# Two transformer blocks on one core: the second block's q, k, conv and gate panels as seven block products ahead of the attention, the conv projection as the attention's filler

## The reference, cut to what matters

```python
h = modulate(rms_norm_2(x, g_pre_mix[l]), sh1, sc1)
proj = h @ w_in[l]                                   # 1024 x 5120
bg, cg, u, q, k, v, ga, gb = jnp.split(proj, split_pts, axis=-1)   # 512 x6, 1024 x2
y_conv = short_conv_branch(bg, cg, u, conv_w[l]) @ w_proj_conv[l]  # bg * conv3(cg * u)
o = stick_breaking_attention(q, k, v)                # 8 heads of 64
y_attn = o @ w_proj_attn[l]
merged = jax.nn.sigmoid(ga) * y_conv + jax.nn.sigmoid(gb) * y_attn
mix_out = merged @ w_out[l]
```

## Time and profile before

| | |
|---|---|
| Median of 3 runs | 2811.23 us |
| Profiled run, and its span | 2811.8 us, 2810.0 us |
| PE busy | 96% of the span, 15746 matmuls |
| DVE, ACT, POOL busy | 62%, 41%, 19% |
| Entry of the second block | 1381.7 to 1471.2 us |
| Attention with filler | 1471.2 to 1879.8 us |
| Gates and projections | 1879.8 to 2059.4 us |

### The profile page before, as it was taken

How to read it: one execution, slowest core, us unless ns; L and a number is a source line. 1 busy time by engine, 2 the same in 40 slices (tenths; PEclk the granted TensorE clock), 3 DMA queues, 4 the chain that set the end, 5 groups by cost and what they waited for, 6 DMA issues and landing times.

```text
span 2810.0 us, 39071 instructions
## 1 busy us (share of the span) xinstructions
PE 2688.0 (96%) x15746; PEld 2169.7 (77%) x15746; DVE 1731.8 (62%) x1998; ACT 1139.4 (41%) x2138; POOL 541.7 (19%) x434
## 2 busy tenths in 40 slices
...
GB/s 134 59 31 18 7 4 24 3 25 178 93 202 188 210 170 193 111 87 99 148 55 46 38 46 31 66 80 51 75 198 102 111 100 120 120 150 120 120 105 120
DMA packets 222604, 269.50 MB, mean 96 GB/s; under 512 B 16455, under 2 KB 158046, under 8 KB 222430
## 3 DMA queue, kind: packets, MB, share of 16 engines
...
...
## 4 chain that ended last, share of the span: by engine, by line
PE 80%; DVE 10%; POOL 3%; ACT 2%; issue 2%; DMA 2%; SPq 0%; ACTq 0%; DVEq 0%; POOLq 0%
PE ps L1647 7%; PE ps L1648 7%; PE ps L1649 7%; PE ps L1702 5%; PE ps L1704 5%; PE ps L1703 5%; PE ps L1761 4%; PE ps L1217 3%; PE ps L1219 3%; PE ps L1218 3%; PE ps L1763 3%; PE ps L1762 3%; PE ps L1438 3%; PE ps L1344 2%; PE ps L1236 1%
## 5 line engine op out<-in xcount | busy, mean ns | idle before, releaser
L1702 PE MATMUL ps<-down_t_hi,down_s_hi 128*128 128x512 f32 x896 | 349.5, 390 | 4.4 <-DVE acc L3205 2.2
L1704 PE MATMUL ps<-down_t_hi,down_s_lo 128*128 128x512 f32 x896 | 348.7, 389 | 0.0
L1703 PE MATMUL ps<-down_t_lo,down_s_hi 128*128 128x512 f32 x896 | 348.6, 389 | 0.0
L1043 POOL TENSOR_SCALAR mean_sq<-ssq 128x1 f32<-128x1 f32 x64 | 37.1, 580 | 1294.7 <-ACT squares_junk_ffn L1921 1242.2
L428 POOL TENSOR_TENSOR slab_lo<-raw,slab_hi 128x1024 fp32r<-128x1024 f32 (+2 forms) x108 | 256.1, 2371 | 9.0
L2385 ACT CAST down_s_hi<-down_a 128x2048 fp32r<-128x2048 f32 x56 | 107.2, 1915 | 370.4 <-PE ps L1704 328.1
L425 POOL TENSOR_SCALAR slab_hi<-raw 128x1024 fp32r<-128x1024 f32 (+2 forms) x108 | 114.6, 1061 | 624.0 <-issue 479.6
L1647 PE MATMUL ps<-act_hi,up_hi 128*128 128x512 f32 (+1 forms) x544 | 205.7, 378 | 6.1 <-issue 2.8
L1648 PE MATMUL ps<-act_lo,up_hi 128*128 128x512 f32 (+1 forms) x544 | 204.9, 377 | 0.0
L1649 PE MATMUL ps<-act_hi,up_lo 128*128 128x512 f32 (+1 forms) x544 | 204.8, 376 | 0.0
L1702 PEld LDWEIGHTS ps<-down_t_hi,down_s_hi 128*128 128x128 f32 x896 | 168.2, 188 | 42.6 <-issue 8.0
...
## 6 DMA issues: line engine op xcount, KB each, us to landing
down_a<-hid_spill SPq DMA_DIRECT2D x32, 1024.0 KB, 7.3
hid_spill<-up_hid ACTq DMA_DIRECT2D x30, 1024.0 KB, 6.4
raw<-in_w_in SPq DMA_DIRECT2D x56, 512.0 KB, 3.8
w_ada<-in_w_ada SPq DMA_DIRECT2D x48, 512.0 KB, 3.9
raw<-in_w_out SPq DMA_DIRECT2D x32, 512.0 KB, 3.8
up_raw<-in_w_up SPq DMA_DIRECT2D x16, 1024.0 KB, 5.4
down_b<-in_w_down SPq DMA_DIRECT2D x16, 1024.0 KB, 6.9
up_raw<-in_w_mlp_in SPq DMA_DIRECT2D x16, 1024.0 KB, 5.4
```

What stands on the lines that cost most here:

```text
L1702: pe.matmul(out, ops["s_hi"][:, k, cols], ops["t_hi"][:, k, :], start=first, stop=False, skip_group_check=True)
L1703: pe.matmul(out, ops["s_hi"][:, k, cols], ops["t_lo"][:, k, :], start=False, stop=False, skip_group_check=True)
L1704: mm = pe.matmul(out, ops["s_lo"][:, k, cols], ops["t_hi"][:, k, :], start=False, stop=last, skip_group_check=True)
```

## The change

The q, k, conv and both gate projections (36 panels, before spread over three stages) become 18 steps of two panels, `IN_COLUMNS`. Each step is seven products of four units (`in_product`), all of them ahead of the attention and behind v. ACT and DVE prepare the weight combinations (`in_high`, `in_low`, `in_add`), six products ahead (`IN_AHEAD`), instead of POOL. Within a step the order is 5, 6, 2, 7 (`UP_FIRST`), with product 1 two places earlier and products 4 and 3 behind the next step's first. The results go to DRAM (`in_d`, `v_d`) and come back for the attention and the merge. The convolution's taps run on DVE inside steps 6 and 7 and steps 9 and 10. The attention's filler is now the conv projection alone (`fill_unit`, 64 units, one for each step from step 10 on); turns alternate between two PSUM banks. After the attention only the attention projection is left.

The diff, cut to PE's, SP's and POOL's parts (`base` columns, orders, loads, products, filler):

```diff
+IN_FIRST = (1, 2, 6, 5, 7)
+IN_COLUMNS = [base + 2 * P * n for base in (IN2_Q, IN2_K) for n in range(2)]
+IN_COLUMNS += [base + 2 * P * n for n in range(2) for base in (CONV2, 2 * CONV2, 0)]
+IN_COLUMNS += [base + 2 * P * n for base in (IN2_GA, IN2_GB) for n in range(4)]
+IN_STEPS = len(IN_COLUMNS)
+IN_CONV, IN_GATES = 4, 10
+IN_KEPT = [u for u in range(IN_STEPS) if not IN_CONV <= u < IN_GATES]
...
+def in_order():
+
+    order = [(0, p) for p in IN_FIRST]
+    for u in range(1, IN_STEPS):
+        order += [(u, 1), (u - 1, 4), (u - 1, 3)] + [(u, p) for p in UP_FIRST[1:]]
+    return order + [(IN_STEPS - 1, 4), (IN_STEPS - 1, 3)]
+
+
+IN_ORDER = in_order()
+IN_TOTAL = len(IN_ORDER)
...
+IN_AHEAD = 6
...
+FILL_FIRST = 10
+FILL_UNITS = KD * 2 * CONV2_PANELS
+FILL_IN_STEPS = FILL_UNITS - 2 * CONV2_PANELS
+
+
+def fill_first_unit(step):
+
+    return min(max(step - FILL_FIRST, 0), FILL_IN_STEPS)
...
-        R5 = Ring(sem, MID_FIRST + len(MID_PANELS), raws[:3], slab_hi[:3], slab_lo[:3], R3)
-        R9 = Ring(sem, 3 * KD, raws[:2], slab_hi[:2], slab_lo[:2], R5)
+        R5 = Ring(sem, 4, raws[:3], slab_hi, slab_lo, R3)
+        R9 = Ring(sem, 2 * KD, raw_half, half_hi, half_lo, R5)
...
+            def in_load(u):
+
+                sp.dma_start(up_raw[u % 2][:], w_in2[:, :, IN_COLUMNS[u]:IN_COLUMNS[u] + 2 * P]).then_inc(sem(f"in_raw{u % 2}"), 16)
...
+            def qkv_loads(i, done):
+
+                for to, src in ((q2[i], in_d[i]), (k2[i], in_d[SB_PAIRS + i])):
+                    sp.dma_start(to[:], src).then_inc(sem(done), 16)
+                sp.dma_start(v2[i][:], v_d[:, :, i * P:(i + 1) * P].rearrange("t p (h e) -> p t h e", e=SB_DIM)).then_inc(sem(done), 16)
...
+            sp.wait_ge(R5.split_done, R5.SLOTS + R5.base + R5.total)
+            in_load(0)
+            sp.wait_ge(sem("v_stored"), FROM["v_stored"] + 32)
+            in_load(1)
+            for u in range(2, IN_STEPS):
+                sp.wait_ge(sem("in_lo"), FROM["in_lo"] + IN_AT[u - 2, 4] + 1)
+                in_load(u)
+            sp.wait_ge(sem("y_stored"), FROM["y_stored"] + 32)
+            for u in (0, 1, 2, 3):
+                in_stored(sp, u)
+            sp.wait_ge(sem("in_lo"), FROM["in_lo"] + IN_AT[IN_STEPS - 2, 4] + 1)
+            qkv_loads(0, "qk_first")
+            for p in range(2):
+                R9.load(sp, 0, p, narrow_view, w_pc[:, :, p * P:(p + 1) * P])
+            sp.wait_ge(sem("in_prod"), FROM["in_prod"] + IN_TOTAL)
             sp.dma_start(y_in[:], y_d.rearrange("c p n -> p c n")).then_inc(sem("y_in"), 16)
...
+            for u in range(IN_GATES, IN_STEPS):
+                in_stored(sp, u)
...
+            for p in range(2):
+                conv_gate_load(p)
+            for i in range(1, SB_PAIRS):
+                qkv_loads(i, "qk_in")
...
+            R5.split(pool, 0, 1, 3)
+            for u in IN_KEPT[-2:]:
+                in_stored(pool, u)
...
+            t_turn("n3", 0, range(KD))
...
+            def v2_part(h, j):
+
+                R5.ready(pe, 0, j)
+                if j == 0 and h == 0:
+                    pe.wait_ge(sem("down_taken"), FROM["down_taken"] + 2 * DOWN_TOTAL)
+                pe.wait_ge(sem("turn_split"), TURNS["n3"] + h * KD + 2 * j + 2)
+                for t in range(4):
...
+            for j in range(3):
+                v2_part(0, j)
+            pe.wait_ge(sem("turn_read"), TURNS["n3"] + KD)
+            t_turn("n3", 1, range(4))
+            v2_part(0, 3)
+            t_turn("n3", 1, range(4, KD))
+            for j in range(4):
+                v2_part(1, j)
...
+            def in_product(n):
+
+                u, p = IN_ORDER[n]
+                slot, b = n % UP_SLOTS, in_bank(u, p)
+                pe.wait_ge(sem("in_lo"), FROM["in_lo"] + n + 1)
+                if u == 0:
+                    if p in (4, 5, 6, 7):
+                        pe.wait_ge(sem("it_lo"), FROM["it_lo"] + IN_T_AT[1, p])
+                    if p in (1, 2, 5):
+                        pe.wait_ge(sem("v2_done"), {1: 5, 2: 6, 5: 7}[p])
...
+                elif p in (6, 7, 4):
+                    pe.wait_ge(sem("in_copied"), FROM["in_copied"] + IN_COPY_AT[u, {6: 1, 7: 6, 4: 7}[p]])
...
+                for k in range(4):
+                    hi, lo = (t_moving(p, w, k) for w in range(2))
+                    pe.matmul(out, up_hi[slot][:, k, :], hi, start=(p in (1, 2, 5) and k == 0), stop=False, skip_group_check=True)
+                    pe.matmul(out, up_hi[slot][:, k, :], lo, start=False, stop=False, skip_group_check=True)
+                    mm = pe.matmul(out, up_lo[slot][:, k, :], hi, start=False, stop=(k == 3), skip_group_check=True)
+                mm.then_inc(sem("in_prod"), 1)
+
+            for n in range(IN_TOTAL):
+                in_product(n)
+
+            def fill_unit(m):
+
+                n, k = divmod(m, CONV2_PANELS)
+                p, h = divmod(n, 2)
+                if m == 0:
+                    pe.wait_ge(sem("c2_split"), CONV2_PANELS)
+                if k == 0 and h == 0:
+                    R9.ready(pe, 0, p)
+                if k == 0 and n:
+                    fill_done(pe, n - 1)
...
+                pe.matmul(ps[:, 5, :], half_hi[p % 2][:, w], y_hi[:, k, cols], start=(k == 0), stop=False)
+                pe.matmul(ps[:, 5, :], half_hi[p % 2][:, w], y_lo[:, k, cols], start=False, stop=False)
+                mm = pe.matmul(ps[:, 5, :], half_lo[p % 2][:, w], y_hi[:, k, cols], start=False, stop=(k == CONV2_PANELS - 1))
...
+                if step >= SB_LAG_TURN:
+                    sb_turn(*divmod(step - SB_LAG_TURN, SB_ITEMS))
...
-                mid_units(unit, end)
+                for m in range(fill_first_unit(step), fill_first_unit(step + 1)):
+                    fill_unit(m)
...
+            for m in range(FILL_IN_STEPS, FILL_IN_STEPS + 2):
+                fill_unit(m)
+            sb_outputs(SB_PAIRS - 1, NT - 1)
+            for m in range(FILL_IN_STEPS + 2, FILL_UNITS):
+                fill_unit(m)
```

and ACT's, DVE's parts:

```diff
+            def in_high(n):
+
+                u, p = IN_ORDER[n]
+                in_slot_free(act, n)
+                if p in (1, 2, 4):
+                    in_loaded(act, u)
+                else:
+                    act.wait_ge(sem("in_sum"), FROM["in_sum"] + IN_SUM_AT[u, p])
+                act.copy(up_hi[n % UP_SLOTS][:], in_source(u, p)).then_inc(sem("in_hi"), 1)
...
+            def v2_take(h):
+
+                for t in range(4 * h, 4 * h + 4):
+                    if t < NT - 1:
+                        act.wait_ge(sem("v2_prod"), t + 1)
+                    else:
+                        R5.panel_done(act, 0, 3)
+                    act.copy(v2_out[h][:, t % 4, :], ps[:, t % 4 if h else 4 + t, :]).then_inc(sem("v2_done"), 1)
+                act.wait_ge(sem("v2_done"), 4 * h + 4)
+                act.dma_start(v_d[4 * h:4 * h + 4].rearrange("t p n -> p t n"), v2_out[h][:]).then_inc(sem("v_stored"), 16)
...
+            v2_take(0)
+            for p in (7, 6, 4):
+                it_hi(1, p)
+            for n in range(4):
+                in_high(n)
+            act.preload_act_table_set("sigmoid_and_others")
+            v2_take(1)
+            for h in range(2):
+                it_hi(h, 5)
+            for n in range(4, IN_AHEAD):
+                in_high(n)
+
...
+            def in_store(u):
+
+                act.wait_ge(sem("in_copied"), FROM["in_copied"] + IN_COPY_AT[u, 4])
+                act.wait_ge(sem("in_out"), FROM["in_out"] + max(IN_OUT_AT[u, p] for p in (2, 5, 3)))
+                if u >= IN_GATES:
+                    act.activation(hid_cols(u, 1, 1), hid_cols(u, 1, 1), ACT.Sigmoid)
+                    act.activation(up_hid[u % 2][:, 0, :], up_hid[u % 2][:, 0, :], ACT.Sigmoid).then_inc(sem("in_gated"), 1)
+                    act.wait_ge(sem("in_gated"), FROM["in_gated"] + u - IN_GATES + 1)
+                act.dma_start(in_d[2 * u:2 * u + 2].rearrange("j p c -> p j c"), up_hid[u % 2][:]).then_inc(sem(f"in_stored{u % 2}"), 16)
...
+            for n, (u, p) in enumerate(IN_ORDER):
+                if p in (1, 6, 7, 4):
+                    in_copy(u, p)
+                if p == 6 and u - 1 in IN_KEPT:
+                    in_store(u - 1)
+                for g in range(2):
+                    if (u, p) == (IN_CONV + 3 * g + 4, 1):
+                        conv_store(g)
+                if n + IN_AHEAD < IN_TOTAL:
+                    in_high(n + IN_AHEAD)
...
+            for u in IN_KEPT[-2:]:
+                in_stored(act, u)
+            for step in range(SB_STEPS + SB_LAG_TURN):
                 sb_step(step)
...
+            for n, (u, p) in enumerate(IN_ORDER):
+                if n and IN_ORDER[n - 1][1] in OUT_AFTER:
+                    in_output(IN_ORDER[n - 1][0], OUT_AFTER[IN_ORDER[n - 1][1]])
+                for x in in_sums(n + IN_AHEAD + 1):
+                    in_add(*x)
+                if n + IN_AHEAD - 1 < IN_TOTAL:
+                    in_low(n + IN_AHEAD - 1)
+                conv_part(u, p)
```

(3 more changed lines are left out.)

654 lines of the change are left out of this document (330 added, 324 removed).

## The result

The changed kernel takes 2821.5 us (median of 7 runs, 2817.98 to 2825.58), the kernel before 2810.86 us in the same comparison. The ratio is 1.0036, with a 95% interval of 1.0026 to 1.0047: slower by 0.36%, 10.6 us. The forecast was 2820.0 us.

What follows compares the result with a forecast made beforehand. PE was taken to bound the kernel, busy 96% of the span. Terms -49.0 + 1.7 + 8.0 + 50.0 - 2.3 gave +8.4 us on the profiled 2811.8; with the median 0.6 lower, 2820 us, 8 in 10 for 2800 to 2840.

Steps and rivals of the forecast that it cites:

- Part 1: Product block ahead of the attention: 504 units in place of 576, 216 matmuls less on PE, -49.0 us.
- Rival E: Product block runs below pace, each us a step costing 18 us: 2838 us; chance 0.12 shared with another slower rival.
- Part 2: Entry, with v now first: its third part waits for POOL's split of the weight slab, +1.7 us, bounds -3 and +6.
- Part 3: First step's third product: PE waits 6.4 us for store, load, cast and copy, then a slower clock; +8.0 us.
- Part 4: Attention without most of its filler: DVE's loop sets the pace, 220 us against PE's 170.0; +50.0 us.
- Handover 10.6: Before the attention's rounds: last product's sum, sigmoids, a 6.4 us store ACT waits for, semaphores, 1.5 until the first scan.
- Rival C: POOL and DMA collide with the attention's loop, last store needing 10 us: 2838 us; chance 0.12 shared with another rival.
- Rounds 190, splits 7, GpSimd 4: Attention loop: 16 rounds of 11.9 us with exposed sigmoids, DVE's hi/lo splits 7 us, POOL splits delaying DVE 4 us.
- Part 5: Merge behind the attention: 64 units remain, idle time falls from 3.8 to 1.5 us; -2.3 us, bounds -4 and +4.
- The rule: Interleaving stages with different limiting engines may gain, so parting attention from filler costs; the opposite view gave about 2762 us.
- A: Rival: sigmoid waits in the attention vanish, a round falls to 9.9 us, 32 us go: 2788 us; chance 0.16.
- B: Rival, no change: smaller pauses at entry, third product and handover store (4 us), POOL costs 0: 2809 us; chance 0.20.

Runs made afterwards that it cites:

- e2: Changed kernel with ACT's sixth operand cast moved behind its first partial-sum copy: 2814.8 us, against the changed kernel's 2821.5.
- e3: Changed kernel with the 2 MB load of the conv output issued behind the wait for the products' last store: 2816.8 us, against 2821.5.
- e1: Changed kernel with DVE writing each tile's mask one item earlier, after the first head of the tile ahead: 2807.6 us, against 2821.5.
- e4: Changed kernel with all 64 conv projection filler units moved behind the attention: 2876.4 us, against 2821.5.
- e9: Kernel with early mask, late cast and later store wait, plus two unread matmuls in each of the attention's first ten steps: 2802.7 us, against 2792.4 without them.

## Why the prediction was right, point by point

**Total.** 2820.0 forecast, 2821.5 measured; +8.4 us forecast on the profiled run. Between the second block's entry and the output projection, the trace shows 688.7 us (1383.9 to 2072.6) for 677.7 before (1381.7 to 2059.4 in the table of before): +11.0. The medians differ by 10.6. The two profiled runs differ by 13.8; the other 2.8 lie in stages that the change doesn't touch (2.2 ahead of the second block, 0.6 behind the merge).

**Part 1, seven products: -49.0.** Right. 288 and 216 units were issued in the block, 504 together, and 504 x 0.681 = 343.2. The block runs from 1453.9 to 1805.2, 351.3 us; of the 8.1 above 343.2, 5.9 are part 3's wait, some 1.4 its clock and 0.8 one later wait for a copy. Rival E falls: 338.23 of 339 us are busy.

**Part 2, the entry: +1.7.** From the first turn of `n3` to the first product it is 1383.9 to 1453.9, 70.0 us; the kernel before had 1449.3 - 1381.7 = 67.6 for the same work. That is +2.4. The reason given holds in its place: PE waits for GpSimd's third split.

```profile
1410.51 1.05 POOL L454 TENSOR_SCALAR slab_hi<-raw 128x1024 fp32r<-128x1024 f32 x1
1411.63 3.19 POOL L457 TENSOR_TENSOR slab_lo<-raw,slab_hi 128x1024 fp32r<-128x1024 f32 x1
```

```profile
1414.88 0.79 PE L1833 MATMUL ps<-slab_hi,act_hi 128*128 128x512 f32 x1 [11.38 <-POOL slab_lo L457]
```

The split's second half took 3.19 us for the 2.37 of the earlier trace rows; these 0.8 us are the difference from the forecast.

**Part 3, the third product: +8.0.** 5.9 of wait for 6.4 forecast. The clock's part is 1.3 by e2 for 1.6. Together 7.2. The sequence forecast (store, load, cast, copy) is the one in the timeline, and e2 took 4.1 of the 5.9 us away.

**Part 4, the attention: +50.0.** 221.6 us of stage for 220, so +51.6. Its terms were less exact than their sum, and that they cancel is luck:
- *Handover 10.6*: 12.7. The mis-sized term is the store: 6.4 taken from the median of the earlier trace rows, 9.2 measured. e3 shows the cause, the 2048 KB load beside it. Rival C had this with 10 us, and I had weighed it too low.
- *Rounds 190, splits 7, GpSimd 4*: 201 forecast; from the first scan to the end of the last multiply, 1818.06 to 2016.17, it is 198.1. The mechanism was right (e1, e4). The exposed waits were 21.3 for the sigmoids and 3.4 at the masks, 24.7 us, for the 16 x 2.6 = 41.6 put into the rounds. The filler's multiplies stand in their place: 13 of them, 9.0 us busy with 3.6 of wait for PE. That they would lie in the waits and cost nothing was forecast, and e4 bears it out: without them the waits are 33.2 + 5.9 = 39.1 us and the loop is as long. So this term was 2.5 (by e4) to 4.4 us too high. Scans and multiplies took 140.0 us for 134.7. With every width at its shortest record they would take 135.0, so the pace was right, and GpSimd's splits cost up to 5.0 us for the 4 forecast, some 2 of them at the loop's first items. DVE's own splits took 8.5 us for 7.
- *End 8.1*: 10.9, from 2016.17 to 2027.02. Among the 2.8 more are two waits of PE for DVE's merges, 1.7 us, that the term did not have.

**Part 5, the merge: -2.3.** 45.6 us (2027.0 to 2072.6) for 43.6 of units leaves 2.0 idle, where before it was 3.8: -1.8.

The sum of the measured parts is -49.0 + 0.8 + 2.4 + 7.2 + 51.6 - 1.8 = +11.2, against the +11.0 read from the stage's ends. The forecast was 2.8 us lower: parts 1, 2, 4 and 5 came out higher by 0.8, 0.7, 1.6 and 0.5 us, part 3 lower by 0.8.

**The rule.** e4 bears on it most closely. Beside DVE's loop 38 us of TensorE's work cost about nothing (195.3 and 194.3 us with and without), and behind it 55 us. The Trainium skill, Perfetto Trace Analysis, Optimization Strategy, says that interleaving regions with different bottlenecks may gain; these rows agree, and give its price here.

**The rivals.** A was the right wish in the wrong kernel: nothing in the changed kernel hides the sigmoids, e1's edit does, and the loop then takes 11.3 us a round (180.6 / 16) and not 9.9, since PE's scores and GpSimd's splits come next. B's quick store exists (4.1 us in e3), but not beside the load. D was the largest miss in what I looked for: the clock was 0.82 in the attention's first quarter and 0.50 in its first 10 us, though the mean of the stage was 0.94. The forecast's sum had no term for this. Since DVE's loop and not PE's work sets the stage (e4), the time held; what the low clock cost through the turns and scores is open (e9).
